# Two woven attention stages: queue orders of ScalarE and VectorE, and where TensorE does turns and values

## What is computed

```python
q_a, kv_a, g_a, q_b, k_b, v_b, q_c, k_c, v_c, f_c = _split_cols(h @ w_in)
o_a = _nsa(q_a, kv_a, g_a, ...)      # 8 heads: compressed, selected and window keys, gated
o_b = _swa_sink(q_b, k_b, v_b, ...)  # 8 heads: keys of a window, with a sink
o_c = _fox(q_c, k_c, v_c, f_c, b_f)  # 8 heads: causal, bias from a cumulated forget gate
g = sigmoid(h @ w_gate + b_gate)     # three gates of width 1024
merged = g[0] * (o_a @ w_br_a) + g[1] * (o_b @ w_br_b) + g[2] * (o_c @ w_br_c)
return merged @ w_out
```

## Time and profile before

| | |
|---|---|
| median of three runs | 2686.55 us (2686.3 to 2687.69) |
| the profiled execution's own time | 2689.6 us |
| its span, first to last instruction | 2687.8 us |
| granted TensorE clock, mean | 0.954 |
| TensorE busy | 2466.6 us (92% of the span) |
| VectorE busy | 1516.8 us (56%) |
| ScalarE busy | 1271.2 us (47%) |
| `attend_and_project`, first layer | 1433 to 1550 us |
| `attend_and_merge`, first layer | 1550 to 1707 us |

### The profile page before, as it was taken

The page is one execution under the profiler, slowest core; times in us unless marked ns, Lnnn a source line. Parts: engine busy times, 40 slices in busy tenths (PEclk is TensorE's granted clock), DMA queues, the critical chain, the costliest instruction groups (busy, mean ns, idle before and its releaser), DMA issues. The chain is left out here.

```text
span 2687.8 us, 46656 instructions
## 1 busy us (share of the span) xinstructions
PE 2466.6 (92%) x17862; PEld 2241.7 (83%) x17862; DVE 1516.8 (56%) x2668; ACT 1271.2 (47%) x1982; POOL 231.8 (9%) x228
## 2 busy tenths in 40 slices
PE   6898779999988889999998899899999988998998
PEld 4677558887777679989987789899899877898998
DVE  4489663343558655655455555555555555665554
ACT  5364652332547554434355455543543554554444
POOL 0023000000003100012000000021021000000220
PEclk8898889999989889999997999999999989999999
DMA  8322022222442125555533234355455442333453
GB/s 319 123 101 73 1 95 94 94 94 94 189 172 95 30 95 183 176 175 187 189 140 126 79 127 157 130 184 188 144 185 188 147 151 72 121 140 141 173 187 109
DMA packets 59959, 367.18 MB, mean 137 GB/s; under 512 B 5872, under 2 KB 17184, under 8 KB 17312
## 3 DMA queue, kind: packets, MB, share of 16 engines
q1 hardware_dynamic: 59664, 365.07, 38.0%
q10 hardware_dynamic: 144, 0.01, 0.0%
HBM read 357.68 MB, written 7.37 MB: 136 GB/s over the span
## 5 line engine op out<-in xcount | busy, mean ns | idle before, releaser
L210 DVE TENSOR_TENSOR w_lo<-ring,w_hi 128x1024 fp32r<-128x1024 f32 x652 | 822.4, 1297 | 606.2 <-ACT w_hi L198 606.1
L252 PE MATMUL psum<-x_hi,w_hi 128*128 128x256 f32 (+1 forms) x3456 | 1070.7, 310 | 58.8 <-DVE x_lo L606 21.9
L253 PE MATMUL psum<-x_lo,w_hi 128*128 128x256 f32 (+1 forms) x3456 | 1056.5, 306 | 0.0
L254 PE MATMUL psum<-x_hi,w_lo 128*128 128x256 f32 (+1 forms) x3456 | 1055.8, 306 | 0.0
L198 ACT ACTIVATE w_hi<-ring 128x1024 fp32r<-128x1024 f32 (+1 forms) x652 | 657.1, 1051 | 302.5 <-PE psum L254 136.4
L252 PEld LDWEIGHTS psum<-x_hi,w_hi 128*128 128x128 f32 x3456 | 678.4, 196 | 98.7 <-issue 62.0
L253 PEld LDWEIGHTS psum<-x_lo,w_hi 128*128 128x128 f32 x3456 | 678.6, 196 | 25.0 <-issue 1.9
L254 PEld LDWEIGHTS psum<-x_hi,w_lo 128*128 128x128 f32 x3456 | 677.6, 196 | 23.3
L1597 PE MATMUL psum<-h_hi,w_hi 128*128 (+1 forms) x640 | 176.7, 276 | 0.0
L1599 PE MATMUL psum<-h_lo,w_hi 128*128 (+1 forms) x640 | 176.7, 276 | 0.0
L1600 PE MATMUL psum<-h_hi,w_lo 128*128 (+1 forms) x640 | 176.7, 276 | 0.0
(11 more groups left out here) (302 smaller groups left out, 3066.4 us busy)
## 6 DMA issues: line engine op xcount, KB each, us to landing
ring<-wstream SPq DMA_DIRECT2D x327, 1024.0 KB, 4.8
kept_hi<-x_hi SPq DMA_DIRECT2D x1, 2048.0 KB, 6.3
kept_lo<-x_lo SPq DMA_DIRECT2D x1, 2048.0 KB, 12.7
x_hi<-kept_hi SPq DMA_DIRECT2D x1, 2048.0 KB, 7.9
x_lo<-kept_lo SPq DMA_DIRECT2D x1, 2048.0 KB, 12.6
rel_bias<-bias_by_distance SPq DMA_DIRECT2D x2, 1024.0 KB, 7.6
na_bias<-rpb SPq DMA_DIRECT2D x4, 438.0 KB, 6.0
cst<-consts SPq DMA_DIRECT2D x1, 1662.0 KB, 11.6
```

What stands on the lines that cost most here:

```text
L210: dve.tensor_tensor(w_lo[:, c % 2, h], ring[:, (c + 2 * i) % RING, h], w_hi[:, c % 2, h].bitcast(F32), ALU.subtract).then_inc(split_done.s ...
L252: pe.matmul(o, w_hi[:, c, w_cols], hi, start=first, stop=False)
L253: pe.matmul(o, w_hi[:, c, w_cols], lo, start=False, stop=False)
L254: return pe.matmul(o, w_lo[:, c, w_cols], hi, start=False, stop=last)
```

## The change

It concerns the two woven stages alone.

- **TensorE.** A step is cut in two: `pe_score` at its old place, ahead of the half chunk, and `pe_rest` (turns and values) in the middle of the half chunk that follows, after 12 of its 24 matmuls. If no half chunk follows, the rest comes just ahead of the next step's scores (`SplitSteps`).
- **ScalarE.** After a step's copy comes the half chunk (`take` and rounding), and only then the step's exponentials (`act_woven`). If a step or an extra comes next and not a half chunk, the exponentials come ahead of that.
- **VectorE.** At a half chunk it makes the split of the half before (`rest_behind`); the last one comes at the stage's end. `take` goes from half 0 to half 1 (but for one chunk of the merging stage).
- **Forget.** Twelve parts, not nine: TensorE makes biases in parts 4, 6, 8 and 10, VectorE takes them out in parts 5, 7, 9 and 11.

```diff
             def pe(self, pe, t):
+                self.pe_score(pe, t)
+                self.pe_rest(pe, t)
+
+            def pe_score(self, pe, t):
                 if t < self.U:
...
                     mm.then_inc(scored.sem, 1)
+
+            def pe_rest(self, pe, t):
                 v = t - self.LAG_T
...
-            def act(self, act, t):
+            def act_turned(self, act, t):
                 v = t - self.LAG_T
...
                                    ACT.Copy).then_inc(turned_sb.sem, 1)
+
+            def act_exp(self, act, t):
                 if t < self.U:
...
-        def pe_half_columns(pe, j, half, hi, lo, kt, place, before=None):
+        def pe_half_columns(pe, j, half, hi, lo, kt, place, middle, before=None):
...
             for n in range(half * CB // 2, (half + 1) * CB // 2):
                 m, k = divmod(n, kt)
+                if n == half * CB // 2 + CB // 4:
+                    middle()
...
-        def pe_half_rows(pe, j, t, cols):
+        def pe_half_rows(pe, j, t, cols, middle):
...
             for k in range(KT):
+                if k == KT // 2:
+                    middle()
...
+        class SplitSteps:
+            def __init__(self, pe, a):
+                self.pe, self.a, self.pending = pe, a, None
+
+            def step(self, t):
+                self.rest()
+                self.a.pe_score(self.pe, t)
+                self.pending = t
+
+            def rest(self):
+                if self.pending is not None:
+                    self.a.pe_rest(self.pe, self.pending)
+                    self.pending = None
+
+        def act_woven(act, a, items, extra, half_chunk):
+            pending = None
+            for what, j, half in items:
+                if pending is not None and what != "half":
+                    a.act_exp(act, pending)
+                    pending = None
+                if what == "step":
+                    a.act_turned(act, j)
+                    pending = j
+                elif what == "extra":
+                    extra(act, j)
+                else:
+                    half_chunk(j, half)
+                    if pending is not None:
+                        a.act_exp(act, pending)
+                        pending = None
+
+        def rest_behind(dve, j, half):
+            q = 2 * j + half - 1
+            if q >= 0:
+                rest_half(dve, g0[0] + q // 2 + 1, 0, q % 2)
...
                         if what == "step":
-                            a.pe(pe, j)
+                            split.step(j)
...
-                    for what, j, half in items:
-                        if what == "step":
-                            a.act(act, j)
-                        elif what == "extra":
-                            forget.act(act, j)
-                        else:
-                            if j and half == 0:
-                                take(j - 1)
-                            round_ahead(act, j, half)
+                    def half_chunk(j, half):
+                        if j and half == 0:
+                            take(j - 1)
+                        round_ahead(act, j, half)
+
+                    act_woven(act, a, items, forget.act, half_chunk)
                     take(n - 1)
...
-                            rest_half(dve, g0[0] + j + 1, 0, half)
-                            if j and half == 0:
+                            rest_behind(dve, j, half)
+                            if j and half == 1:
                                 take(j - 1)
+                    rest_behind(dve, n, 0)
                     take(n - 1)
...
-                        rest_half(dve, g0[0] + j + 1, 0, half)
-                        if j and half == 0 and j != last_proj + 1:
+                        rest_behind(dve, j, half)
+                        if j and half == 1 and j != last_proj + 1:
                             take(j - 1)
                         if (j, half) == (last_proj, 1):
                             y_lower(0, slice(0, 4))
+                    rest_behind(dve, n, 0)
...
-            PARTS = 9
+            PARTS = 12
...
-                if part > 4:
-                    for h in range(2 * part - 10, 2 * part - 8):
-                        dve.wait_ge(read.sem, self.rb + 2 * part - 8)
+                if part > 4 and part % 2:
+                    for h in range(part - 5, part - 3):
+                        dve.wait_ge(read.sem, self.rb + part - 3)
...
-                if 4 <= part < 8:
-                    pe.wait_ge(step.sem, self.b + 9)
-                    pe.wait_ge(mixed.sem, self.m0 + 4 * (part - 4))
-                    for h in range(2 * part - 8, 2 * part - 6):
+                if part >= 4 and part % 2 == 0:
+                    if part == 4:
+                        pe.wait_ge(step.sem, self.b + 9)
+                    else:
+                        pe.wait_ge(mixed.sem, self.m0 + 2 * (part - 4))
+                    for h in range(part - 4, part - 2):
```

More of the change, by code:

```diff
@@ L830, in _ @@
                     for t in range(a.length):
-                        a.act(act, t)
+                        a.act_turned(act, t)
+                        a.act_exp(act, t)
             stored.n += 32 if bring_back else 0
@@ L1796, in _ @@
                     hi, lo = model_operand(S)
+                    split = SplitSteps(pe, a)
                     for what, j, half in items:
                         if what == "step":
-                            a.pe(pe, j)
+                            split.step(j)
                         elif what == "extra":
@@ L1804, in _ @@
                             if kind == "r":
-                                mm = pe_half_rows(pe, j, half, o.shape[2])
+                                mm = pe_half_rows(pe, j, half, o.shape[2], split.rest)
                             else:
-                                mm = pe_half_columns(pe, j, half, hi, lo, KT, lambda m: acc(j, S, S * m))
+                                mm = pe_half_columns(pe, j, half, hi, lo, KT, lambda m: acc(j, S, S * m), split.rest)
                             if half:
@@ L1902, in _ @@
                                                  lambda m: projected(j, m // 2)[:, m % 2 * S:m % 2 * S + S],
-                                                 operand_made)
+                                                 split.rest, operand_made)
                         elif kind == "out":
@@ L1908, in _ @@
                             apart = 512 if j == n - 1 else S
-                            mm = pe_half_columns(pe, j, half, hi, lo, KT, lambda m: acc(j, S, apart * m), y_made)
+                            mm = pe_half_columns(pe, j, half, hi, lo, KT, lambda m: acc(j, S, apart * m), split.rest, y_made)
                         else:
-                            mm = pe_half_columns(pe, j, half, hi, lo, KT, lambda m: acc(j, S, S * m))
+                            mm = pe_half_columns(pe, j, half, hi, lo, KT, lambda m: acc(j, S, S * m), split.rest)
                         if half:
@@ L1937, in take, with half_chunk @@
                             y_upper(slice(6, 8))
-                    for what, j, half in items:
-                        if what == "step":
-                            a.act(act, j)
-                            continue
+                    def half_chunk(j, half):
                         if j and half == 0:
@@ L1949, in _ @@
                             y_upper(slice(0, 4))
+                    act_woven(act, a, items, None, half_chunk)
                     moments.act(act, g0[0] + n + 1)
```

## The result

The changed kernel takes 2666.75 us (median of four runs, 2665.55 to 2667.7) beside 2687.12 for the kernel before: a ratio of 0.9922, 95% interval 0.9907 to 0.9938, that is 20.4 us or 0.8% less. I forecast 2680 us and a range from 2671 to 2691. The direction was right, the size was three times too small, and the time lies outside the range. The profiled execution took 2667.57 us, with a span of 2665.8; that of before was 2687.8, so 22.0 us are to be found between the two traces.

What follows compares the result with a forecast made beforehand. TensorE, 92% busy, was taken as the bound, with gains only where it idles or runs at half clock. Per layer 1.7 (waits less costs) + 3.1 (clock) - 1.65 (merging stage) = 3.15, twice 6.3: 2680 us, range 2671 to 2691.

Steps and rivals of the forecast that it cites:

- Forget parts: Projecting stage: spread over twelve, TensorE's three waits for VectorE's bias go, 6.9 us per layer.
- Waits after: Projecting stage: TensorE's idle time after the change is 7.9 us instead of 11.2, 3.3 saved per layer.
- Clock: Projecting stage: two stretches at half clock (1.2 instead of 2.4 GHz) instead of four, 3.1 us saved per layer.
- the fall at `c_col`: Projecting stage: TensorE's wait for `c_col` stays, growing from 0.85 to 1.8 us, with a half-clock stretch still expected.
- a wait alone will do it: Merging stage: one 2.0 us wait and mean clock 0.99 hint that a wait suffices for a half-clock stretch.
- The case of no low stretch: Rival: no half-clock stretch left in the projecting stage, 12.7 us saved in all, 2674 us; chance 0.12.
- Cost of the cuts: Both stages: halves cut in the middle cost 0.09 us for each of 14 steps, 1.3 us a stage.
- stalls: Merging stage: later exponentials and `take` make TensorE wait 0.35 us, bounds 0 and 5.
- Slower: Rival: VectorE falls behind in the merging stage, 9.4 us lost in all, 2692 us; chance 0.12.
- The change doesn't do what it says: Rival: turns in the half's middle still wait, the 1.2 us stay, 2683 us; chance 0.07.
- The falls of its own that the merging stage might have got: Rival: cut halves bring two half-clock stretches per merging stage, 6.4 us in all, 2686.5 us; chance 0.04.
- One sign of being wrong: A merging stage below 157 us would mean that switches cost nothing.

Runs made afterwards that it cites:

- before_f12_behind: The kernel before with twelve forget parts and VectorE's new order, whole steps on TensorE and ScalarE: 2675.23 us (0.9951).
- after_steps_whole: The changed kernel, but TensorE does a step whole again in both stages: 2674.2 us (0.995).
- after_rows_midwait: The changed kernel, but for the projecting stage's last two chunks TensorE asks for the split's upper half only in the middle of the first half: 2661.74 us (0.9903).
- after_merge_old: The changed kernel, but the merging stage goes by the old orders on all three engines: 2667.35 us (0.9926).
- the fill kernel: The kernel before with twelve forget parts and dummy matmuls on TensorE ahead of the scores of steps 3 and 6 in the projecting stage: 2668.38 us (0.9924).

## Why the prediction was wrong, point by point

- **Forget parts: right.** The waits of 6.9 us went; alone, the edit shortens the stage by 6.4.
- **Waits after: right, and nearly in size.** Forecast 1.8 at `c_col`, 1.4 at scores, 1.3 and 3.4 at the two row chunks, none at turns: 7.9. Measured 1.7, 1.4, 0.9 and 3.1: 7.1, so 4.1 saved instead of 3.3. The order of each queue, written out step by step, gave these numbers.
- **Clock: the step that failed.** I counted on two low stretches in the projecting stage where one came, and on no change in the merging stage where one went. At 1.6 us each, three that went are 4.8 per layer where I had 3.1, so 1.7 more, and the merging stage's is 1.5: 6.4 of the miss. The price of a low stretch was right (1.5 to 1.7 measured), though the rows that I read it from give 1.4 and, for forget matmuls, 1.24; the places were wrong. I let the fall at `c_col` stay, because I took from the merging stage that "a wait alone will do it". It has no fall behind its 1.7 us, and that wait of 2.0 has one in 16 of 28 cases. I let one fall go with the forget waits; with these waits gone it stayed at its place, behind two small waits. And that the merging stage's fall went is luck as far as the runs show. The case of no low stretch (2674 us, chance 0.12) was the nearest of the rivals, and still short.
- **Cost of the cuts: mis-sized.** I took 1.3 us a stage for fourteen cuts and 0.3 for the last split. A stage's length without its waits and with 1.6 us off for each low stretch is 99.6 us before, 100.0 in before_f12_behind, after_steps_whole and the changed kernel, and 100.1 in after_rows_midwait: some 0.4 us, not 1.6, and none of it between whole steps and cut ones. In the merging stage it is 0.9 (after_merge_old), where I had 1.3 and 0.35 for stalls of which the view of waits shows none. A part of what I left out can be seen: four turns that stand behind a half take 0.60 us here, behind a score 0.66, which gives back 0.06 of each cut's 0.09. Against that, a half starts 0.55 us after its score in the changed kernel, and a turn 0.52 us after its score in the kernel before (medians of the merging stage; I had 0.55 for both). In sum that is 0.06 a step and 0.8 for the fourteen.

```profile
1621.88 0.60 PE L704 MATMUL psum<-cst,prob 128*128 128x128 f32 x4
```

- **Rivals.** "Slower" did not come: VectorE kept up in the merging stage. "The change doesn't do what it says" is out, no turn waits. The falls of its own that the merging stage might have got did not come either; its clock is 1.00. One sign of being wrong did come, a merging stage below 157 us, but it did not mean that switches cost nothing: they took 0.9 us, and the low stretch that stayed away gave 1.5. The Trainium skill, "TensorE: Matmul & The Clock Gate", section "A second HAM failure mode: psum-queue depth-cycling", tells of a clock that goes up and down because TensorE pauses briefly and often between groups of matmuls. Cuts that cost 0.09 us or less brought nothing of the kind here (clock 1.00); the pauses of 0.3 to 1.1 us in the step pairs are nearer to what it tells of, and there the fill kernel agrees with it (clock 1.00 where two of them were filled).
- **The sum.** Per layer I had 3.15 and the traces show 9.15. The 6.0 between them are 0.8 from waits, 3.2 from clock, 1.2 from cuts in the projecting stage and 0.75 from cuts and stalls in the merging stage. Two layers make 12.0 us of the miss; the rest of it, to the 22.0 between the profiles, is the 3.7 us outside the stages.
- **The range** was too narrow by the clock alone. I had four low stretches per projecting stage in hand and one in the merging stage, 16 us in two layers, and no row that told what started them; I should have let all of them go at the low end. The 2677 to 2683 that I gave "with its bounds" is not worked out from them either: with every bound at its good end my own sum gives 2661.

What stays open: what sets whether a wait of 1 to 3 us is followed by a fall. The runs show that pauses come ahead of the falls and that the same pause can pass without one. They don't show the rule, nor whether it is the pause or the work missing in it that counts.

## What to carry to other kernels

A stage with waits and a clock that falls has two accounts, and they need not be settled by the same edit: here taking out the largest waits (6.9 us) gave their own length and nothing more, while small ones of 0.3 to 1.1 us were followed by falls that cost 1.6 each. Filling a pause with matmuls that nobody reads is a cheap way to learn which pauses may be the ones. And edits to the queues of several engines are one edit: with the split one half behind, the cut on TensorE took 1.8 us off the projecting stage (110.4 to 108.7); without it, the same cut with ScalarE's new order, made the stage 11 us longer than with whole steps (110.8 to 121.8).

## What the runs showed of the hardware that I had not expected

- Spare matmuls in TensorE's pauses made the kernel 7.4 us faster (2675.8 to 2668.4), by three low stretches of 1.6 us per layer, less the 1.5 to 2 us per layer that the fill took too long.
- Four falls of the clock at the same offsets (12.5, 26.2, 39.8, 53.5 us, to 0.1 in the first layer) with and without 6.9 us of waits that lay at the fourth of them and behind it.
- The same code with the same 2.0 us wait at clock 0.50 behind it or at 1.00, 16 to 12 in 28 cases, worth 1.5 us each time. Over two layers, two kernels can differ by 3 us in this stage without differing in its code.
